# Late conditioning rows on the vector engine, and latent values with squares in the differential drain

## The reference, cut to what matters

```
mod = silu(c) @ ada_w + ada_b                    # 1024 x 3072 weights, one row
shift, scale, gate = split(mod, 3)
h = rms_norm(x) * (1 + scale) + shift
proj = h @ w_in                                  # c_q, c_kv, k_pe, na, diff, gates
kv = rms_norm(c_kv) @ w_ukv                      # keys and values of the latent attention
o_mla, o_na, o_d = latent, neighbourhood and differential attention
o_d = rms_norm(o_d, subln_g) * (1 - lam_init)    # needs the squares of o_d
x = x + gate * (concat(o * silu(g)) @ w_out)
```

## Time and profile before

| what | us |
|---|---|
| median of 3 executions (their range) | 4284.48 (4276.0 to 4285.75) |
| the profiled execution | 4271.69 |
| its span | 4269.9 |
| PE, DVE, ACT, POOL busy | 4107.0, 1943.4, 1566.7, 552.0 |
| mean granted TensorE clock | 0.981 of full speed |

### The profile page before, as it was taken

The page is one execution under the profiler, slowest core; times in us unless marked ns, Lnnn a source line. Parts: engine busy times, 40 slices in busy tenths (PEclk is TensorE's granted clock), DMA queues, the critical chain, the costliest instruction groups (busy, mean ns, idle before and its releaser), DMA issues.

```text
span 4269.9 us, 53415 instructions
## 1 busy us (share of the span) xinstructions
PE 4107.0 (96%) x22404; PEld 3089.1 (72%) x22404; DVE 1943.4 (46%) x2772; ACT 1566.7 (37%) x2408; POOL 552.0 (13%) x654
## 2 busy tenths in 40 slices
PE   7999989999999989999999799999999999999999
PEld 5776556777776556787833668888888888888887
DVE  3336956434336956433345743333334443333344
ACT  4326855323326855323356333121123231211231
POOL 0010111100010111110068810000002210000010
PEclk8999999999999999999999999999999999999999
DMA  4111000251111000032100101111111101111111
GB/s 161 58 62 43 1 1 1 89 188 50 58 62 43 1 1 1 21 111 69 40 11 1 43 30 50 50 50 50 50 50 70 40 20 50 50 50 50 50 65 64
DMA packets 47055, 208.33 MB, mean 49 GB/s; under 512 B 14688, under 2 KB 15328, under 8 KB 25568
## 3 DMA queue, kind: packets, MB, share of 16 engines
q1 hardware_dynamic: 31568, 144.98, 9.8%
q10 hardware_dynamic: 15248, 59.94, 3.9%
HBM read 188.12 MB, written 12.58 MB: 47 GB/s over the span
## 4 chain that ended last, share of the span: by engine, by line
PE 87%; DVE 6%; ACT 3%; issue 2%; DMA 1%; POOL 0%; ACTq 0%; DVEq 0%; POOLq 0%
PE ps L734 14%; PE ps L1305 13%; PE ps L1307 13%; PE ps L1306 13%; PE ps L1080 3%; PE ps L964 3%; PE ps L966 3%; PE ps L965 3%; PE ps L821 2%; PE ps L838 2%; PE ps L1036 2%; PE ps L1133 1%; PE ps L1021 1%; PE ps L1122 1%; PE ps L790 1%
## 5 line engine op out<-in xcount | busy, mean ns | idle before, releaser
L1305 PE MATMUL ps<-n_hi,w_hi 128*128 128x512 f32 x1280 | 500.1, 391 | 0.0
L1307 PE MATMUL ps<-n_hi,w_lo 128*128 128x512 f32 x1280 | 498.0, 389 | 0.0
L1306 PE MATMUL ps<-n_lo,w_hi 128*128 128x512 f32 x1280 | 498.0, 389 | 0.0
L1305 PE MATMUL ps<-m_hi,w_hi 128*128 128x512 f32 x1152 | 449.8, 390 | 0.0
L1307 PE MATMUL ps<-m_hi,w_lo 128*128 128x512 f32 x1152 | 448.2, 389 | 0.0
L1306 PE MATMUL ps<-m_lo,w_hi 128*128 128x512 f32 x1152 | 448.1, 389 | 0.0
L1451 ACT ACTIVATE w_hi<-w 128x2048 fp32r<-128x2048 f32 x103 | 196.9, 1912 | 443.0 <-DMA w<-in_wstream 442.8
L2106 DVE TENSOR_TENSOR w_lo<-w,w_hi 128x2048 fp32r<-128x2048 f32 x103 | 235.9, 2290 | 177.6 <-ACT w_hi L1451 177.6
L2016 ACT ACTIVATE arena<-ps 128x512 f32<-128x512 f32 x128 | 76.5, 598 | 585.3 <-PE ps L1307 585.3
L2826 DVE TENSOR_TENSOR m<-ps,arena 128x512 f32<-128x512 f32 x128 | 88.5, 692 | 433.5 <-ACT arena L2016 433.5
L1305 PEld LDWEIGHTS ps<-n_hi,w_hi 128*128 128x128 f32 x1280 | 240.3, 188 | 50.9 <-issue 1.2
(11 more groups left out here) (393 smaller groups left out, 8142.5 us busy)
## 6 DMA issues: line engine op xcount, KB each, us to landing
w<-in_wstream SPq DMA_DIRECT2D x121, 1024.0 KB, 4.8
arena<-in_wstream ACTq DMA_DIRECT2D x17, 1024.0 KB, 5.2
out<-h ACTq DMA_DIRECT2D x48, 256.0 KB, 2.0
h<-in_na_bias ACTq DMA_DIRECT2D x6, 1152.0 KB, 6.7
h<-in_xT SPq DMA_DIRECT2D x2, 2048.0 KB, 12.5
m<-in_wstream SPq DMA_DIRECT2D x4, 1024.0 KB, 16.4
arena<-in_wstream SPq DMA_DIRECT2D x4, 1024.0 KB, 23.7
h<-in_xT ACTq DMA_DIRECT2D x4, 1024.0 KB, 10.6
```

The source lines that it names most:

```text
L1305: mm(dst, wb[0][:, k, wcols], hi[:, k, :], start=(g == 0), stop=False)
L1306: mm(dst, wb[0][:, k, wcols], lo[:, k, :], start=False, stop=False)
L1307: last = mm(dst, wb[1][:, k, wcols], hi[:, k, :], start=False, stop=(g == KT - 1))
```

## The change

It has two parts.

**A, conditioning rows.** The 16 late products leave PE and ACT's copies go with them. DVE makes a row itself, with 8 chained instructions of 128x256: `row = sum over k of block[k] * c_silu[k]`, each partition its own partial sum, so that the sum over partitions on PE stays. Rows are made behind items 3 to 29, the sums follow 1 to 4 items later and up to item 31, the reads move from items 7, 19, 25 to 13, 26, 31, ACT's loads hang on the rows, and there are 3 row buffers in place of 2. The table load of layer 1 moves from item 8 to 15. The second `wide_c` goes.

**B, latent values and squares.** Four of the eight latent value matmuls, with their copies, move into rounds `U-1 .. U+2` of the differential drain (banks 0 and 1, twice), so the factors' transposes move to banks 2 and 3; the other four stay first in `latent`. The square of the differential output's first half moves to ACT's round `U+1`; that of the second half moves to POOL, first in its latent part. Both layers have this.

```diff
-ADA_MAIN_AT = {2 + 3 * i // 2: i for i in range(len(ADA_LATE))}
-ADA_SUM_AT = {at + 1: i for at, i in ADA_MAIN_AT.items()}
-ADA_READ_AT = {7: 0, 19: 1, 25: 2}
+ADA_ROW_AT = {at: i for i, at in enumerate((3, 5, 7, 9, 12, 14, 16, 18, 19, 20, 22, 23, 24, 26, 27, 29))}
+ADA_SUM_AT = {at: i for i, at in enumerate((6, 8, 10, 12, 16, 17, 19, 20, 21, 22, 24, 25, 28, 29, 30, 31))}
+ADA_READ_AT = {13: 0, 26: 1, 31: 2}
+ADA_ROWS = 3
-ADA_SUM_AT_FOUR = 8
+ADA_SUM_AT_FOUR = 15
...
# PE
+            def latent_v(layer, t):
+                if t in (2, 3, 4, 5):
+                    pe.wait_ge(sems["lat_v_done"], NT * layer + t - 1)
+                mm(ps[:, t % 2 if t < 4 else t - 4, 0:384], lt_kv[:, t * P:t * P + P], lt_wv, start=True, stop=True)\
+                    .then_inc(sems["lat_v_full"], 1)
             def latent(layer):
-                pe.wait_ge(sems["lat_w"], 128 * (layer + 1))
-                for t in range(NT):
-                    mm(ps[:, t, 0:384], ...)
+                for t in range(4, NT):
+                    latent_v(layer, t)
...
-                        if layer == 0 and i in ADA_MAIN_AT:
-                            late = ADA_MAIN_AT[i]
...
-                            ada_products(ada_slots[late % ADA_SLOTS], 6)
...
+                        if c == U - 1:
+                            pe.wait_ge(sems["lat_w"], 128 * (layer + 1))
+                            pe.wait_ge(sems["exp_done"], T.since("exp_done", 2 * U - 1))
+                        if c in (U - 1, U + 1):
+                            for v in range(2):
+                                latent_v(layer, 2 * (c > U) + v)
                         if c == U + 1:
...
-                                factor_turns(LAT_PAIRS - 1, hf, hf)
+                                factor_turns(LAT_PAIRS - 1, hf, 2 + hf)
...
# ACT
-                    if layer == 0 and i in ADA_MAIN_AT:
-                        late = ADA_MAIN_AT[i]
-                        ada_row(ADA_FIRST + late, 6)
-                        if late + ADA_SLOTS < len(ADA_LATE):
-                            ada_load(late + ADA_SLOTS)
+                    if layer == 0 and i in ADA_SUM_AT and ADA_SUM_AT[i] + ADA_SLOTS < len(ADA_LATE):
+                        act.wait_ge(sems["ada_row"], ADA_FIRST + ADA_SUM_AT[i] + 1)
+                        ada_load(ADA_SUM_AT[i] + ADA_SLOTS)
...
-                for hp in range(2):
-                    nc.scalar.activation(m[:, hp, :], m[:, 6 + hp, :], ACT.Square).then_inc(sems["lat_d_act"], 1)
...
+                        if c in (U, U + 2):
+                            for v in range(2):
+                                latent_v(layer, 2 * (c > U) + v)
+                        if c == U + 1:
+                            act.wait_ge(sems["o_free"], T.since("o_free", NT))
+                            nc.scalar.activation(m[:, 0, :], m[:, 6, :], ACT.Square).then_inc(sems["lat_d_act"], 1)
...
# DVE
+            def ada_row(late):
+                count = ADA_FIRST + late
+                row, wb = ada_rows[:, count % ADA_ROWS, :], ada_slots[late % ADA_SLOTS]
+                dve.wait_ge(sems[f"ada_late{late % ADA_SLOTS}"], 16 * (late // ADA_SLOTS + 1))
+                dve.wait_ge(sems["ada_sum"], count + 1 - ADA_ROWS)
+                for k in range(KT):
+                    col = c_silu[:, k:k + 1]
+                    if k == 0:
+                        V.tensor_scalar(row, wb[:, k, :], col, None, ALU.mult).then_inc(sems["v_link"], 1)
+                    elif k < KT - 1:
+                        V.scalar_tensor_tensor(out=row, in0=wb[:, k, :], scalar=col, in1=row, op0=ALU.mult, op1=ALU.add)\
+                            .then_inc(sems["v_link"], 1)
+                    else:
...
+                            .then_inc(sems["ada_row"], 1)
+                    if k < KT - 1:
+                        dve.wait_ge(sems["v_link"], T.next("v_link"))
...
                     if layer == 0 and i in ADA_READ_AT:
                         modulation_read(i)
+                    if layer == 0 and i in ADA_ROW_AT:
+                        ada_row(ADA_ROW_AT[i])
...
# POOL
+                G.tensor_tensor(out=m[:, 1, :], in0=m[:, 7, :], in1=m[:, 7, :], op=ALU.mult).then_inc(sems["lat_d_act"], 1)
                 for p in range(LAT_AHEAD):
                     squares_sum(p)
```

More of the change, by code:

```diff
@@ L630, in build @@
         lay_ring, at = region(arena, 14 * S, 2, HALF)
-        ada_rows, at = region(arena, at, 2, BW)
+        ada_rows, at = region(arena, at, ADA_ROWS, BW)
         c_wide, at = region(arena, at, KT, 32)
@@ L873, in differential_sums @@
                 last.then_inc(sems["lat_d_t"], 1)
+            def latent_v(layer, t):
[3 more added lines that the diff above has]
+                    .then_inc(sems["lat_v_full"], 1)
             def latent(layer):
-                pe.wait_ge(sems["lat_w"], 128 * (layer + 1))
-                for t in range(NT):
-                    mm(ps[:, t, 0:384], lt_kv[:, t * P:t * P + P], lt_wv, start=True, stop=True)\
-                        .then_inc(sems["lat_v_full"], 1)
+                for t in range(4, NT):
+                    latent_v(layer, t)
                 for p in range(LAT_AHEAD + 1):
                     if p < LAT_AHEAD:
-                        pe.wait_ge(sems["lat_v_done"], NT * layer + min(p, 3) + 1)
+                        pe.wait_ge(sems["lat_v_done"], NT * layer + 4 + min(p, 3) + 1)
                         if p >= 4:
@@ L939, in ada_sums @@
                 for j in range(2):
-                    last = mm(ps[:, 7, at + j:at + j + 1], ada_rows[:, count % 2, j * P:j * P + P], ones[:, 0:1],
+                    last = mm(ps[:, 7, at + j:at + j + 1], ada_rows[:, count % ADA_ROWS, j * P:j * P + P], ones[:, 0:1],
                               start=True, stop=True)
@@ L973, in layer_end @@
                             ada_sums(ADA_FIRST + late, 2 * late)
-                        if layer == 0 and i in ADA_MAIN_AT:
-                            late = ADA_MAIN_AT[i]
-                            pe.wait_ge(sems[f"ada_late{late % ADA_SLOTS}"], 16 * (late // ADA_SLOTS + 1))
-                            if late == 0:
-                                pe.wait_ge(sems["lat_m_done"], 2 * LAT_PAIRS)
-                                pe.wait_ge(sems["c_wide_done"], 2)
-                            else:
-                                pe.wait_ge(sems["ada_row"], ADA_FIRST + late)
-                            ada_products(ada_slots[late % ADA_SLOTS], 6)
                         if layer == 0 and i == LAM_AT:
-                            pe.wait_ge(sems["ada_row"], ADA_FIRST + len(ADA_LATE))
                             lam_sums(1)
@@ L1476, in ada_row @@
                     act.wait_ge(sems["ada_sum"], count - 1)
-                nc.scalar.activation(ada_rows[:, count % 2, :], ps[:, bank, 0:BW], ACT.Copy).then_inc(sems["ada_row"], 1)
+                nc.scalar.activation(ada_rows[:, count % ADA_ROWS, :], ps[:, bank, 0:BW], ACT.Copy).then_inc(sems["ada_row"], 1)
             def ada_load(late):
@@ L1621, in gate_input, with latent_v @@
                 nc.scalar.activation(half(n_hi_h, u // 2, u % 2), half(n, u // 2, u % 2), ACT.Copy).then_inc(sems["lay_hi"], 1)
+            def latent_v(layer, t):
+                act.wait_ge(sems["lat_v_full"], NT * layer + t + 1)
+                nc.scalar.activation(lt_v[:, t, :], ps[:, t % 2 if t < 4 else t - 4, 0:384], ACT.Copy)\
+                    .then_inc(sems["lat_v_done"], 1)
             def latent(layer):
-                for t in range(NT):
-                    act.wait_ge(sems["lat_v_full"], NT * layer + t + 1)
-                    nc.scalar.activation(lt_v[:, t, :], ps[:, t, 0:384], ACT.Copy).then_inc(sems["lat_v_done"], 1)
-                for hp in range(2):
-                    nc.scalar.activation(m[:, hp, :], m[:, 6 + hp, :], ACT.Square).then_inc(sems["lat_d_act"], 1)
+                for t in range(4, NT):
+                    latent_v(layer, t)
                 for p in range(LAT_AHEAD + 1):
@@ L2179, in layer_end @@
                 parts_done[0] += 16
-                if layer == 0:
-                    wide_c()
                 def gated_low(i):
```

2 lines of the change are left out of this document (1 added, 1 removed).

## The result

The change makes the kernel faster, by about 0.6%.

A forecast was written before the change was run, and what follows sets the result against it. TensorE, busy 96% of the span, was taken as the bound. Part A 19.2 - 1.1 - 3.5 = 14.6 us plus part B 7.0 gave 21.6 off 4284.5, so 4262.9 us; range 4248 to 4277.

The forecast's parts named there:

- 19.2 off PE: Layer 0's end: removing the 16 late products takes 19.2 us off PE, 1.2 each; the sums stay.
- A row at 3.9 alone, 4.9 under POOL's addition: DVE's eight-instruction row in layer 0's end: 3.9 us among the gates, 4.9 among the outputs, where POOL adds.
- 67 us of DVE against 84 of PE: Layer 0's end, items 16 to 29: DVE's work totals 67 us while PE takes 84, so it fits.
- Lambda wait 1.1: Behind item 26 PE's lambda sums wait for DVE's read, addition and product: 1.1 us lost.
- Join 3.5: Layer 0's end to next projection: last row lengthens DVE's chain, 3.5 us lost, bounds 2.5 and 5.5; PE idle some 6.
- 16 x 0.5: Layer 0's end: PE time kept for the 16 remaining sums, 0.5 us each, subtracted from the 27.7 us.
- The clock at the join: First item after the join: longer idle time may bring the lower clock earlier, up to 1.5 us, taken as 0.
- Part B 3.5 a layer: Latent start: 2.7 from values plus 1.9 from squares less 1.1 in the drain, 3.5 us a layer, bounds 2.5 and 4.5.
- rival 1: Layer 0's end: DVE lags with rows at 5.9 us, stalling PE 4 us plus 3 at the join; 4270 to 4273; chance 0.12.
- 2: Latent start: part B gives nothing because the chain is held elsewhere; 4269.9 us; chance 0.05.
- 4: Layer 0's end: another wait, such as the weight stream, fills PE's room; 4275 to 4277 us; chance 0.05.
- 3: Layer 0's end: DVE becomes the bound; all gain gone at rows of 8.4 us, 1.05 an instruction; chance 0.04.

The follow-up runs named there:

- rows of half length: The changed kernel with four instructions per late row instead of eight, leaving out half of the terms: 4243.67 us, ratio 0.9922.
- doubled rows: The changed kernel with every late row computed twice, 16 instructions in place of 8: 4293.34 us, ratio 1.005.
- B alone: The kernel before with only the edits of part B, the late products staying on PE: 4264.54 us, ratio 0.9981.
- last row at 28: The changed kernel with the last row made behind item 28 instead of 29 and the last three loads issued earlier: 4255.03 us, ratio 0.9949.
- values: Part A plus, of part B, only the four values moved; both squares stay on ACT at the latent start: 4258.51 us, ratio 0.996.
- both again: Second measurement of the changed kernel with lambda product behind item 25, last row behind item 28 and its last three loads earlier: 4243.07 us, ratio 0.9936.

## Why the prediction was right

The forecast was 4262.9 us, 21.6 less than the median of three executions; measured were 4250.57, inside the range and 12 us below the forecast. The places of the change give 22.7. From the profiled execution the same sum leads to 4250.1, and that execution came at 4248.88. That so near a hit was made is in part luck: the second pair of profiles differs by 15.2 only, and in the first pair stages without an edit moved by up to 2.5 us one way and 1.8 the other. By places:

- **19.2 off PE.** The items fell by 18.36 with 1.0 of lambda wait in them (item 26 to 27 takes 6.95 us where it took 5.98): 19.3. Right.
- **A row at 3.9 alone, 4.9 under POOL's addition.** The instructions take 483 to 485 ns and the last row 4.8 us in all. Right: alone a row takes 4.0 us, under an addition 4.9 (once 5.1). In these two rows of the changed kernel DVE and POOL start together and end within 0.15 us of each other:

```profile
953.63 1.45 DVE L2163 TENSOR_SCALAR arena<-arena,c_silu 128x256 f32<-128x256 f32 x1 [0.22 <-DVE gain L2150]
953.64 1.29 POOL L2938 TENSOR_TENSOR arena<-arena 128x512 f32<-128x512 f32 x1 [1.37 <-ACT arena L1464]
```

  An instruction of 346 ns became one of 1445, 1.1 us more; in the middle of a row it is 0.91 (485 to 1399). This is the exclusive lock of the Trainium skill, "SBUF — State Buffer", section "Who interferes with whom": the trace agrees, in that one instruction in each such row ends 0.15 to 0.3 us behind POOL's. The full 1.3 that the rule would put on a row at most was never reached. The prediction counted seven of the eight instructions as exposed; the row above is the eighth, with one SBUF tensor, and it was held up as well. And of the ten rows among the outputs seven met an addition, not all ten, so 67 us was a little high.
- **67 us of DVE against 84 of PE, so the rows are hidden.** Right, and shown by the rows of half length: the items don't move. The 17 us of room are an average, though: doubled rows met PE at single places long before the sum was used up.
- **Lambda wait 1.1.** Measured 0.90 idle, 1.0 in the pitch. Right, and taken away it came back in the items (183.17). The prediction had it and the wait for the last load as separate terms, and had that load late by up to 1 us, 0.6 in the sum. In the changed kernel it was not late (5.13 us from issue to landing, 0.3 us to spare); in one version, where it took 6.4, it was late by 1.05.
- **Join 3.5.** From item 29's addition to the low parts: forecast 15.4, measured 15.5 (970.94 to 986.43), though made up otherwise: no load wait (0.6 in the sum), a row of 4.8 for 3.9 and tiles of 5.38 for 6.42, since POOL's addition held up the row in place of a tile, and a wait of 1.03 for ACT's `n_hi_m` that the sum didn't have. But what PE lost is not this difference. The sums behind items 29 to 31 stand on PE beside DVE's chain, 1.0 us of them between the addition of item 29 and the end of the items, and the prediction had charged them already in 16 x 0.5. So PE's loss at the join is 5.12 - 2.59 = 2.5 us, and its wait 4.62, not "some 6". **This is the step that was off**: 1.0 counted twice. Part A gives 15.8 where 14.6 was forecast.
- **The clock at the join.** "Up to 1.5 more" for a longer idle time: the changed kernel's first matmul after it runs at 0.77 us where it was 0.47 with the shorter wait, but the whole stage to the neighbourhood scores is the same (250.99 and 251.12). With the join shortened the stage takes 250.1 to 250.5, so it can't have cost more than 0.9 us. A cost of its own isn't shown: rows of half length start at 0.47 us too, and their stage takes 253.3, with other stretches at the lower clock in it.
- **Part B 3.5 a layer.** Measured 3.44: values 1.61 (2.7 - 1.1), squares 1.85 (1.9). The barrier comes 0.98 us later (last differential score to it 12.59 before, 13.57 now) where 1.1 was forecast. POOL's square took 1.89, not 2.36, and was covered. Right in each term. Whether it arrives at the end is less clear. The latent loop took 224.2 to 224.4 us in the changed kernel with 10.2 us at the lower clock at its start (6.8 + 3.4), against 223.0 to 223.2 with 6.8 before. With the same part B it also took 221.2 with 3.4 us at the lower clock (B alone, layer 0) and 223.2 with 6.8 (rows of half length). So up to 1.2 us a layer is given back in some executions and 2 us gained in others, and what decides that is open. That A and B add up in the stages and not in the medians is also open: six executions that spread over 5 to 25 us don't rank kernels 5 us apart.
- **The level.** The text set 21.6 off the median of three, 4284.48, and so named 4262.9. Of the two levels it had, the profiled execution's was the one at which the kernel before runs: the five later measurements of it gave 4270.64 to 4275.48. That is why the time came 12 us below the forecast, at the lower end of the range, with the gain right to 1.1.
- **The rivals.** 1, 2 and 4 are refuted by the stages (no stall among the items but the lambda wait, 3.44 a layer in part B). Of rival 1 the late load behind item 20 came true, 2.5 us of it, and PE lost nothing by it. 3 put the break-even at rows of 8.4 us; doubled rows, 8 to 9 us, lose 47.3 us in the items and the join (35.9 + 11.4), where that sum gives some 29 at 9 us. The mechanism was right and the break-even too far away: the last load's wait is 7.2 of the difference, and the stalls at the gate items are 7.0 (four pitches of 8.26, 5.9, 8.1 and 7.55 us where the changed kernel has 5.58, 5.8, 5.58 and 5.8). Some 4 us of the difference stay open. Late rows make late loads, and gates have a tight cover too.
- **The range.** Its lower end was set with 23.5 us for "the better bounds". The bounds given for the terms add up to 24.6 (15.6 in part A, 4.5 in each layer of part B), so it should have stood at 4247; the measured time is inside either.

## What to carry to other kernels

A vector engine with half its time free can take work off TensorE at no price as long as each piece fits under the item it stands behind; the price is at the joins, where nothing of TensorE's is left to hide it. So put the last piece one item earlier, and issue its load earlier too. When a wait is removed and nothing comes of it, look at what the next instruction waited for, and whether that wait belongs to the edit at all: here it was a load that took 1.3 us longer in that one trace, and the gain was there once the load had room. And compare places in two traces, not medians, when the effect is a few us and a few us of clock come and go.

## What the runs showed of the hardware

The granted clock falls to its lower level, 1.2 GHz, for stretches of 3.4 to 27.3 us, in much the same places in every profile but with other lengths, and each place has its own few values: 127.9, 129.6 or 131.1 us for the same differential scores. The one that comes and goes as a whole is in a part that no edit touched. In three of the profiles (last row at 28, values, and both again) TensorE ran there at the lower level for 27.3 us, in the other eleven not at all. The same place of the program in the changed kernel and, 10 us earlier by the span's start, in the version with both edits (second profile):

```profile
3414.00:3421.00 7.00, 5.95 (x38) 5.19 (x37) 1.74 (x3) 0.69 (x1) 0.00 (x0) 1.00 0.00 0
3421.00:3449.00 28.00, 28.00 (x178) 24.57 (x177) 16.86 (x21) 15.70 (x24) 9.25 (x7) 1.00 0.01 1
```

```profile
3404.00:3411.00 7.00, 5.95 (x38) 5.19 (x37) 1.75 (x3) 0.69 (x1) 0.00 (x0) 1.00 0.00 0
3411.00:3439.00 28.00, 28.00 (x122) 26.29 (x121) 11.77 (x17) 11.05 (x18) 8.91 (x7) 0.51 0.00 1
```

PE is busy for all 28 us at a granted clock of 0.51 and gets 122 matmuls through instead of 178. Ahead of the fall it had been idle for 1.05 of 7 us. The changed kernel has the same 1.05 us of idle time at this place (5.95 of 7 busy), and its clock stays up. From the end of layer 1's items to the end of the program the three took 2348 to 2351 us, the others 2334 to 2339: at least twice what the two edits together brought. What decides it is open.
